# Moving the low weight tiles by 64 bytes in the local memory of a two-block network kernel

## The reference

```python
def first_block(x, c, ...):            # depth 1
    mod = silu(c) @ w_ada + b_ada      # six vectors: shift, scale, gate, twice
    u = rms_norm(x, ln1) * (1 + scale1) + shift1
    x = x + gate1 * mixer_sublayer(u, w_in, ...)   # conv branch and SSM scan branch
    u2 = rms_norm(x, ln2) * (1 + scale2) + shift2
    x = x + gate2 * (square(relu(u2 @ w_up)) @ w_down)      # d_ff 4096
    return rms_norm(x, final_norm)

def second_block(x, ...):
    x = x + 0.5 * swiglu(rmsnorm(x, g_ffn1), w1_gate, w1_up, w1_down)   # d_ff 2816
    p = rmsnorm(x, g_mix) @ w_in
    ...                                # indexed sparse attention and latent attention
    x = x + concatenate([out_a, out_b]) @ w_out
    x = x + 0.5 * swiglu(rmsnorm(x, g_ffn2), w2_gate, w2_up, w2_down)
    return rmsnorm(x, g_final)
```

## Time and profile before

| | |
|---|---|
| runs | 2295.84, 2296.09, 2298.12 us; median 2296.09 |
| span of the profiled execution | 2287.7 us |
| TensorE matmul busy | 2237.3 us, 98% |
| weight loads busy | 1829.0 us, 80% |
| VectorE, ScalarE busy | 1320.4 us (58%), 863.7 us (38%) |
| mean DMA rate | 97 GB/s |
| granted TensorE clock | 0.993 of full speed |

### The profile page before, as it was taken

How to read it: one execution, slowest core, us unless ns; L and a number is a source line. 1 busy time by engine, 2 the same in 40 slices (tenths; PEclk the granted TensorE clock), 3 DMA queues, 4 the chain that set the end, 5 groups by cost and what they waited for, 6 DMA issues and landing times.

```text
span 2287.7 us, 28544 instructions
## 1 busy us (share of the span) xinstructions
PE 2237.3 (98%) x10872; PEld 1829.0 (80%) x10872; DVE 1320.4 (58%) x1835; ACT 863.7 (38%) x1223; POOL 4.5 (0%) x8
## 2 busy tenths in 40 slices
PE   7999999999999999999999999999989899999998
PEld 5888888887888888888878888889868667888887
DVE  5577777777673475433475344355777766434344
ACT  5655555543222342322342222234445444212124
POOL 0000000000000000000000000000000000000000
PEclk9999999999999999999999999999999899999999
DMA  7323233224543243323222222223121002232321
GB/s 263 114 75 105 96 98 104 92 74 162 169 154 103 92 129 115 101 90 99 92 92 92 92 92 93 92 92 91 49 65 38 19 32 79 92 97 96 103 83 65
DMA packets 208140, 222.08 MB, mean 97 GB/s; under 512 B 9413, under 2 KB 200330, under 8 KB 205994
## 3 DMA queue, kind: packets, MB, share of 16 engines
q1 hardware_dynamic: 206362, 210.26, 28.5%
q10 hardware_dynamic: 1680, 10.49, 1.1%
HBM read 218.57 MB, written 2.16 MB: 96 GB/s over the span
## 4 chain that ended last, share of the span: by engine, by line
PE 87%; DVE 7%; ACT 3%; issue 2%; DMA 1%; ACTq 0%; DVEq 0%
PE G L551 24%; PE G L552 24%; PE G L553 24%; PE G L587 2%; PE G L589 2%; PE G L588 2%; DVE wlo L1806 1%; PE X L739 1%; ACT whi L1159 1%; PE G L1024 1%; DMA araw<-in_w_ada 1%; PE X L1041 1%; PE X L1007 1%; PE X L1031 1%; DVE score L2688 1%
## 5 line engine op out<-in xcount | busy, mean ns | idle before, releaser
L551 PE MATMUL G<-ahi,whi 128*128 128x512 f32 x1496 | 603.0, 403 | 4.1 <-DVE alo L2782 1.4
L552 PE MATMUL G<-alo,whi 128*128 128x512 f32 x1496 | 592.2, 396 | 0.0
L553 PE MATMUL G<-ahi,wlo 128*128 128x512 f32 x1496 | 591.9, 396 | 0.0
L1806 DVE TENSOR_TENSOR wlo<-raw,whi 128x2048 fp32r<-128x2048 f32 x176 | 403.3, 2292 | 240.2 <-ACT whi L1159 236.9
L1159 ACT ACTIVATE whi<-raw 128x2048 fp32r<-128x2048 f32 x176 | 335.5, 1907 | 454.9 <-PE G L553 434.3
L551 PEld LDWEIGHTS G<-ahi,whi 128*128 128x128 f32 x1496 | 282.9, 189 | 72.3 <-issue 2.4
L553 PEld LDWEIGHTS G<-ahi,wlo 128*128 128x128 f32 x1496 | 282.6, 189 | 67.2
L552 PEld LDWEIGHTS G<-alo,whi 128*128 128x128 f32 x1496 | 282.9, 189 | 66.7 <-issue 2.2
L551 PE MATMUL G<-hhi,whi 128*128 128x512 f32 x784 | 310.2, 396 | 0.7 <-DVE wlo L1806 0.7
L552 PE MATMUL G<-hlo,whi 128*128 128x512 f32 x784 | 309.6, 395 | 0.0
L553 PE MATMUL G<-hhi,wlo 128*128 128x512 f32 x784 | 309.5, 395 | 0.0
(11 more groups left out here) (410 smaller groups left out, 2783.6 us busy)
## 6 DMA issues: line engine op xcount, KB each, us to landing
raw<-in_w_in SPq DMA_DIRECT2D x43, 1024.0 KB, 5.1
raw<-in_w_up SPq DMA_DIRECT2D x38, 1024.0 KB, 5.3
raw<-in_w_down SPq DMA_DIRECT2D x32, 1024.0 KB, 5.1
raw<-in_w_gate SPq DMA_DIRECT2D x22, 1024.0 KB, 5.1
braw<-in_w_ada SPq DMA_DIRECT2D x12, 1024.0 KB, 5.1
raw<-in_w_in SPq DMA_DIRECT2D x20, 512.0 KB, 4.5
araw<-in_w_ada ACTq DMA_DIRECT2D x8, 1024.0 KB, 17.7
bc<-acum_dram SPq DMA_DIRECT2D x8, 1024.0 KB, 6.9
```

The source lines that it names most:

```text
L551: pe.matmul(bank[:], wh[:, j, f], rh[:, j, :], start=(j == 0), stop=False)
L552: pe.matmul(bank[:], wh[:, j, f], rl[:, j, :], start=False, stop=False)
L553: last = pe.matmul(bank[:], wl[:, j, f], rh[:, j, :], start=False, stop=(j == k - 1))
L1806: tt(wlo[s][:], raw[s][:], r32(whi[s][:]), ALU.subtract).then_inc(lo_split, 1)
```

## The change

Two pads of 16 fp32 (64 bytes in each partition) are named, one ahead of the two low weight tiles and one behind them. Nothing reads or writes them.

```diff
         raw = [fixed(f"raw{s}", [P, UNIT]) for s in range(2)]
         whi = [fixed(f"whi{s}", [P, UNIT], F32R) for s in range(2)]
+        fixed("pad_w", [P, 16])
         wlo = [fixed(f"wlo{s}", [P, UNIT], F32R) for s in range(2)]
+        fixed("pad_x", [P, 16])
         xT = fixed("xT", [P, KB, T])
```

## The result

The changed kernel takes 2284.33 us (median of 8 runs, 2277.29 to 2287.61) against 2295.97 us (8 runs, 2287.80 to 2298.12) for the kernel before. The ratio is 0.9953, with a 95% interval of 0.9939 to 0.9968: 10.8 us less, 7 to 14. So the change makes the kernel faster, by about half a percent. Of all executions in this study two stood far off and are left out of the ratios: 3685.83 us of the kernel before (mean clock 0.554) and 9785.62 us of the kernel whose activations move by 256 bytes.

What follows compares the result with a forecast made beforehand. The prediction took the number of TensorE matmuls times the distance between their starts as the bound. Its terms, -13.7 - 1.7 + 0.4 = -15.0 us, took the median from 2296.1 to 2281 us, with 2265 to 2304 for 8 in 10.

Steps and rivals of the forecast that it cites:

- What bounds the kernel: Long products: 7512 TensorE matmuls of 512 columns at about 233 ns, 1750 us, 77% of the span.
- The size: ahi, hhi, bhi: 1.95 ns less on 7032 matmuls, 13.7 us; yhi 1.7 us less; chi 0.4 us more.
- The step that failed: Activations behind the second pad move by 128 bytes; taken as 0 if places count modulo 128, left as a doubt.
- even and odd: Operand places as even or odd multiples of 64 bytes, taken to decide the distance between matmul starts.
- crossed pair: A moving operand and the stationary one loaded beside it, one even and one odd; each was to save 5.85 ns.
- chi's 11.7 ns: chi triples before the change: two crossed pairs of three, taken to save 3 x 3.9 = 11.7 ns.
- Rival 1: Long products: addresses of the low weights don't matter, time stays at 2296 us; chance 0.16.
- Rival 2: Long products: chi's whole saving on all 7032 matmuls, 28.7 us less in all, 2267 us; chance 0.25 of the forecast's 0.62.
- Rival 3: Long products get slower as line 552 locks on long durations of 398 to 404 ns; 2303 to 2308 us; chance 0.22.
- milder end: Rival 3 with line 552 at 398 ns: 3 ns in a triple, 7.0 us more, given as 2303 us.
- yhi gain: yhi's 128 triples go from 233.3 to 229.0 ns a matmul, 1.7 us less.
- The Trainium skill's rule: TensorE has two independent read ports, so loading weights takes nothing from the running matmul; time would stay at 2296 us.

Runs made afterwards that it cites:

- the control: Against the kernel before, only a 256-byte pad behind the low weights, moving all activations by 256 bytes; 2292.04 us, ratio 0.9989.
- the first experiment: Against the kernel before, only the first pad, moving low weights and all activations by 64 bytes against the high weights; 2279.72 us, ratio 0.9944.

## Why the prediction was right in its number and wrong in its reason

**What bounds the kernel**: held. TensorE has 88% of the chain that ended last, 87% before, VectorE and ScalarE kept their durations and their waits, and a shorter distance between starts came through: 7032 x (232.9 - 231.2) = 12.0 us for ahi, hhi and bhi, 384 x (233.2 - 229.7) = 1.3 for yhi, 96 x 3.3 = 0.3 the other way for chi, 13.0 in all, against 11.6 in the medians and 10.8 by the ratio.

**The size**: 231.0 ns was forecast and 231.2 came; for yhi 229.0 and 229.7; for chi 233.3 and 232.3. By these the prediction looks as if its mechanism were shown. It isn't.

**The step that failed** is "Everything behind the second pad moves by 128 bytes. If places count modulo 128, this is 0." Placement repeats every 256 bytes and not every 128, shown by the control and by the move of 128. In the rows of before the distances of the long products were 128 and 192 alone; even and odd put these in one class each with 0 and 64, which no row had. So the change had two parts, not one:
- the activations by 128 bytes, by itself 226.7 ns and 2258 us;
- the low weights by 64 bytes, by itself 233.3 ns and 2298 us, no gain.

Together they give 231.2. The low part's move, which the change is named for and to which the prediction gave the whole gain, takes back some 26 of the 37 us that the other part brings. With the failed step falls the one on it: one crossed pair saves 5.85 ns. The kernel with exactly that crossed pair and the activations in place modulo 256 saved nothing, and a kernel with no crossed pair had the full effect. That half of chi's 11.7 ns, spread over three matmuls, gave 1.95 ns where 1.7 was measured is luck: the distances come in few values, and the same one is reached from many placements.

**The rivals.** Rival 1, that the low weights' address doesn't matter, is false as said (26 us in company of the activations' move), and true to 0.3% of the low weights moved alone; the forecast and it both overlooked the activations. Rival 2 didn't come. Rival 3 had its signs: one line of the triple did lock on long durations, 397 against 389 and 392, but the other two fell by more. Its last sentence, that the move by 128 of the activations would act if it counts, was the right doubt with the wrong sign. Its milder end, 2303, is 2296.1 + 7.0 without the yhi gain that its middle, 2308, has taken off; with it, it would be 2301.

**The Trainium skill's rule** that the load of the next weights takes nothing from the running matmul ("TensorE: Matmul & The Clock Gate", "Step-by-step: what each phase is for") speaks against any effect of placement. This case's traces do not agree: the distance between starts of ahi and hhi goes from 226.7 to 233.3 ns with the placement alone, 6.6 ns on each matmul.

**What stays open** is the law. Distance between the moving operand and the weights loaded beside it does not explain all: chi before and ahi in the first experiment have the same such distances, 192, 128, 192, and run at 229.0 and 231.1; yhi in the changed kernel and chi with the activations moved by 128 bytes share 64, 0, 64 and run at 229.7 and 233.3; and both low parts moved together don't return to 226.7. In both pairs the moving operand of chi changes its place from one matmul to the next and the other's does not. That may be the missing part, but it helps in the first pair and costs in the second, and it was not tried by itself. Nor was a common move of all tiles: the high weights stood at 128 throughout, so distance is told apart from place only through the low weights.

That it is the weight load with which the stream collides is not shown: no kernel ran the same stream without loads. There is evidence for it. With all activations at 128, the place of the low weights alone takes the distance from 226.7 (at 128) to 231.2 (at 192 or 0). In this stream only weight loads read that tile. VectorE writes it, but left no mark on the durations at 226.7.

## What to carry to other kernels

Where a kernel is a long row of like matmuls, the placement of its operands modulo 256 bytes is a free parameter. Here it was worth 3% of each matmul of 512 columns, and one pad of 128 bytes gave 1.7% of the whole kernel. Try moving and stationary operands at the same place modulo 256, and measure a few others: it was the best place for long rows of 512 columns that all started alike, and not for 256 columns or for chi. When a pad is put in for one tensor, everything behind it moves too; test the two moves apart, and put in a control that moves all by the supposed period. A forecast that meets its number has not thereby met its reason: the experiment that undid half of the change was the one that told.

## What the runs showed of the hardware

- In the long stretches of ahi and hhi the distance between starts of fp32r matmuls with 512 columns took only a few values: 226.7, 228.9, 231.1 and 233.3 ns, and one mixed kind of 232.3 to 232.5. chi reached 235.5 in one kernel. Three times each is 680.0, 686.7, 693.3, 700.0 and about 706.7, so a triple changes in steps of 6.67 ns. At a granted clock of 1.00, 2.4 GHz, that is 16 cycles. What the step is made of is not shown.
- With all operands at the same place modulo 256, 512 columns took 226.7 ns, the least seen, and 256 columns 119.7 ns with the roles swapped, against 113.7 with the activations 64 bytes further on.
- With activations at 0 and both weight parts at 128 modulo 256, two steady patterns exist, 232.3 and 233.3 ns, and a stretch keeps the one that it falls into: the same program, same tiles, 997 us and 1184 us into the run.
- A run's time moved with its mean clock. In the kernel before, a line through its runs gives 1.7 to 2.0 us for 0.001 in each of the three sets; in the others, with 4 to 10 runs each, 1.0 to 2.7. The profiles place it in the attention stage, in which TensorE waits. A single profiled execution can hide a difference of 0.5%; here the attention stage alone was 6.8 us longer in the faster kernel.
